# Norm sums as columns of numbers, spread to rows by TensorE, and a longer share of a convolution on VectorE

## The chip, the cores and the metric

The kernel runs on one core of a Trainium2 chip. The metric is the time of one execution in microseconds (us) on the device; a kernel is described by the median of its runs. A profiled execution is one more run, of which the hardware recorded every instruction. Its time is that of the whole run; its span, from the first to the last recorded work, is a little shorter.

## What is computed

Two blocks, each of two layers, on one sequence of 256 tokens with 1,024 features, all in float32. The change touches the seam between the blocks and the first mixer of the second block. Cut to that:

```python
# end of the first block: x = x + gate*y, then
x = rmsnorm(x, final_norm_g)              # per token: x / sqrt(mean(x*x)+eps) * g
# second block, layer 0
h = rmsnorm(x, norm_mix_g[0])             # again a norm per token, of the result above
p = h @ w_in_ab                           # 512 columns a, 512 values v, 512 gates g
ya = fnet_heads(p[..., :512], fnet_map)   # DFT over tokens and head, real part, a map
u = v * sigmoid(g)
u = conv(u, conv_w, 31 taps, pad 15, one filter per channel) + conv_b
u = silu(layernorm(u, per head of 128))   # four heads
y = concat([ya, u]) @ w_out_ab
x = x + y                                 # then the SwiGLU layer, and the second layer
```

## The kernel before

**Layout.** Activations lie with features on the 128 partitions and tokens along the row: a tile is 128 x 256, a tensor of 1,024 features is eight tiles `d`. In the second block's residual path the tokens lie on the partitions instead. Weights come as 128 x 2048 slabs (1 MB) by DMA into five `raw` buffers. ScalarE copies a slab to a rounded high half and VectorE subtracts to get the low half, both into one of four `W` buffers; each product is then three TensorE matmuls (high x high, high x low, low x high) on the rounded type. `stream` and `fill(k)` are the calls that do this splitting: `fill(k)` brings the engine up to slab k + 3 of the list of matrices. It stands by hand in the programs of ScalarE and VectorE, and a slab's split can't start before the slab four places ahead of it has been used up.

**Order.** There is no scheduler. Each engine has its own program, written out by hand, and runs it strictly in order; semaphores tie them together. `Port.wait_ge` drops waits already met. A matmul of plain float32 has two records in the trace, one of the rounded type has one. A PSUM bank (`pb0` to `pb7`) may be written when the name before it in that bank is free: `Outputs` hands out banks in a ring (`out`, `hold`) or by hand (`place`), and `freed(name)` says which semaphore frees it. `bank_free` on TensorE waits for that.

**The seam.** After the attention output (`project("ao", ...)` on VectorE) the first norm needs the sum of squares over all features of each token. ScalarE squares each tile, VectorE adds the eight squares (`add`), and TensorE multiplies with a matrix of ones (`row_sum`), so that all 128 partitions get the sum as a row of 256; ScalarE takes the root (`row_root`) and VectorE the reciprocal (`row_close`) of 128 x 256. `col_sums` gives the same sums as a column. Then X is scaled by gain and norm (eight operations, `s_x3`), squared and summed again for the second norm. Meanwhile TensorE already works on the unnormed product: `head(20, ...)` and `head(22, ...)` are slabs 20 to 23 (outputs `b` 0 to 7, gates and values), with the closing of the two sums (`close`) between the halves of each. Slabs 24 and 25 give `a` 0 to 3.

**The convolution.** Four tiles `d`, 31 taps. VectorE does taps as multiply-adds of 128 x 256 (`pump`), in the order of the list `taps`; the first tap of a tile is ScalarE's (`start_tap`). `NPE` taps of tile 2 and all of tile 3 are matmuls on TensorE (`convolved`) with diagonal matrices that ScalarE makes (`diagonals`). On TensorE the DFT matmuls (`ac`, `f`, `fm`) stand ahead of them. VectorE's `low(R1, h, fm)`, one for each of the four `fm` outputs, stands in the middle of the taps and counts up `s_flo`. Then each tile is normed per token: `ln_mean`, `ln_centre`, `ln_square`, `ln_var`, `ln_root`, `ln_scale`. `mixed` is the product with `w_out_ab`, `turn` a transpose of its sum.

## Time and profile before

| | us |
|---|---|
| median of 3 runs | 755.68 |
| lowest, highest | 754.87, 759.08 |
| the profiled execution, its own time | 755.56 |
| its span | 753.8 |
| TensorE matmuls busy | 721.7 (96%) |
| VectorE busy | 503.9 (67%) |
| ScalarE busy | 389.9 (52%) |

The share of an engine over the whole span is a mean over stages. In the stage that the change touches, from about 246 to 345 us of the span, all three engines have to be read beside each other, instruction by instruction. In a timeline a row gives the start, the length from first start to last end, engine, line of the code, operation, output <- inputs, shapes and the count of equal instructions that follow each other. Matmuls overlap in the pipeline, so what one costs is the distance between starts, not its length.

### The profile page before, as it was taken

How to read it: one execution, taken by the hardware profiler on the slowest of the kernel's cores; microseconds unless marked ns; L12 is line 12 of the kernel's file. 1: busy time of each engine (PE TensorE's matmuls, PEld its weight loads, DVE VectorE, ACT ScalarE, POOL GpSimd, SP SyncE). 2: the span in 40 equal slices, each digit the busy share in tenths (PEclk: the TensorE clock that was granted, in tenths of full speed). 3: DMA queues.
4: the chain of work that ended last, by engine and by line, in shares of the span. 5: the costliest groups of instructions: out<-in, count | busy, mean ns of one | idle time of the engine just before them, and what ended most of it. 6: DMA issues, size and time to landing. Idle time of an engine off the chain costs nothing.

```text
span 753.8 us, 9658 instructions
## 1 busy us (share of the span) xinstructions
PE 721.7 (96%) x3900; PEld 629.7 (84%) x3900; DVE 503.9 (67%) x760; ACT 389.9 (52%) x602; POOL 2.4 (0%) x8
## 2 busy tenths in 40 slices
PE   3999995999999999999999999999999999999996
PEld 2888885999999999888888888888888888888885
DVE  4866987986976789987664454555576554454444
ACT  4146526347675667846844434444466533434423
POOL 0000000000000000000000000000000000000000
PEclk9999998999999999999999999999999999999998
DMA  9999774796934434234364555545324455545201
GB/s 348 418 420 422 324 270 177 296 423 272 400 124 169 167 130 184 79 113 168 142 249 171 200 187 184 206 168 196 139 113 171 181 206 171 203 184 179 102 0 57
DMA packets 23085, 156.65 MB, mean 208 GB/s; under 512 B 2560, under 2 KB 2688, under 8 KB 5120
## 3 DMA queue, kind: packets, MB, share of 16 engines
q1 hardware_dynamic: 22464, 153.41, 53.6%
q0 software_dynamic: 576, 2.62, 1.0%
q8 instruction: 31, 0.51, 0.3%
q14 instruction: 14, 0.11, 0.0%
HBM read 154.97 MB, written 1.05 MB: 207 GB/s over the span
## 4 chain that ended last, share of the span: by engine, by line
PE 77%; DVE 10%; ACT 8%; DMA 3%; issue 1%; SPq 0%; DVEq 0%; ACTq 0%
PE pb L1454 19%; PE pb L1456 18%; PE pb L1455 18%; PE pb L1524 13%; DVE w L956 4%; PE pb L1683 2%; DVE raw L959 2%; DMA raw<-w_dram 2%; ACT w L593 2%; PE pb L1784 1%; ACT r L698 1%; ACT t L701 1%; PE pb L1530 1%; DVE rs L1015 1%; PE pb L1714 1%
## 5 line engine op out<-in xcount | busy, mean ns | idle before, releaser
L956 DVE TENSOR_TENSOR w<-raw,w 128x2048 fp32r<-128x2048 f32 x97 | 221.4, 2291 | 142.6 <-ACT w L593 142.5
L593 ACT ACTIVATE w<-raw 128x2048 fp32r<-128x2048 f32 x97 | 184.8, 1913 | 157.2 <-PE pb L1456 114.9
L1454 PE MATMUL pb<-w,r 128*128 128x512 f32 (+1 forms) x640 | 244.2, 381 | 0.7 <-DVE r L959 0.3
L1456 PE MATMUL pb<-w,r 128*128 128x512 f32 (+1 forms) x640 | 241.0, 377 | 0.0
L1455 PE MATMUL pb<-w,r 128*128 128x512 f32 (+1 forms) x640 | 240.6, 376 | 0.0
L1454 PEld LDWEIGHTS pb<-w,r 128*128 128x128 f32 x640 | 120.5, 188 | 23.1 <-issue 1.8
L1456 PEld LDWEIGHTS pb<-w,r 128*128 128x128 f32 x640 | 120.4, 188 | 22.5
L1455 PEld LDWEIGHTS pb<-w,r 128*128 128x128 f32 x640 | 120.6, 188 | 21.2
L1454 PE MATMUL pb<-r,w 128*128 128x256 f32 x352 | 101.6, 289 | 7.1 <-DVE r L956 6.6
L1455 PE MATMUL pb<-r,w 128*128 128x256 f32 x352 | 100.2, 285 | 0.0
L1456 PE MATMUL pb<-r,w 128*128 128x256 f32 x352 | 100.1, 284 | 0.0
L959 DVE SCALAR_TENSOR_TENSOR raw<-raw,acc 128x1024 f32<-128x1024 f32 x64 | 75.0, 1221 | 3.1 <-DMA raw<-w_dram 3.0
L1454 PEld LDWEIGHTS pb<-r,w 128*128 128x128 f32 x352 | 68.1, 194 | 8.1 <-issue 7.1
L1455 PEld LDWEIGHTS pb<-r,w 128*128 128x128 f32 x352 | 68.2, 194 | 0.1
L1456 PEld LDWEIGHTS pb<-r,w 128*128 128x128 f32 x352 | 68.1, 194 | 0.0
L1524 PE MATMUL pb<-h,ow 128*128 128x256 f32 x256 | 57.3, 387 | 3.5 <-ACT h L656 3.5
L1524 PEld LDWEIGHTS pb<-h,ow 128*128 128x128 f32 x256 | 49.7, 195 | 11.0 <-issue 3.9
L897 ACT ACTIVATE t<-pb,rn 128x256 f32<-128x256 f32 x44 | 20.7, 475 | 59.8 <-PE pb L1456 59.8
L959 DVE SCALAR_TENSOR_TENSOR f<-f,vec 128x256 f32<-128x256 f32 x102 | 42.4, 483 | 5.0 <-ACT f L661 4.6
L959 DVE SCALAR_TENSOR_TENSOR t<-pb,rn,t 128x256 f32<-128x256 f32 x44 | 21.1, 483 | 22.9 <-ACT t L897 22.9
L1524 PE MATMUL pb<-t,ow 128*128 128x256 f32 x128 | 27.8, 379 | 0.0
L1524 PEld LDWEIGHTS pb<-t,ow 128*128 128x128 f32 x128 | 24.3, 190 | 3.3
(174 smaller groups left out, 572.0 us busy)
## 6 DMA issues: line engine op xcount, KB each, us to landing
raw<-w_dram SPq DMA_DIRECT2D x129, 1024.0 KB, 4.9
ow<-w_dram SPq DMA_DIRECT2D x8, 1024.0 KB, 19.2
ow<-w_dram SPq DMA_DIRECT2D x8, 512.0 KB, 15.6
oh<-w_dram SPq DMA_DIRECT2D x2, 1024.0 KB, 21.5
x<-x_dram SPq DMA_DIRECT2D x2, 512.0 KB, 6.0
f<-rc_dram POOLq DMA_DIRECT2D x1, 1024.0 KB, 5.1
acc<-row_dram POOLq DMA_DIRECT2D x2, 512.0 KB, 5.4
out_dram<-f SPq DMA_DIRECT2D x4, 256.0 KB, 2.3
```

The costliest lines, as they stand in the source:

```text
L593: return e.activation(out, in_, ACT.Copy, **kw)
L698: e.activation(hi_of(R, kt), F3[:, kt, :], ACT.Identity, **kw).then_inc(done, 1)
L701: e.activation(tt[kt][:, :], F3[:, kt, :], ACT.Identity, **kw).then_inc(done, 1)
L897: e.activation(tt[(at_ - 1) % 4][:, :], bank_of("gu", layer, i, a)[:, 0:T], ACT.Silu, scale=rn[:, 2 * layer, a:a + 1]).then_inc(s_sgt, 1)
L956: return e.tensor_tensor(out, a, b, op)
L959: return e.scalar_tensor_tensor(out, a, s, b, op0, op1, **kw)
L1015: e.reciprocal(RS[{0: 0, 1: 1, 2: 0, 3: 1, 4: 0, 6: 1, 7: 0}[i]][:, :], root[:, :]).then_inc(s_rs, 1)
L1454: e.matmul(out, a_hi, b_hi, start=start, stop=False)
L1455: e.matmul(out, a_hi, b_lo, start=False, stop=False)
L1456: return e.matmul(out, a_lo, b_hi, start=False, stop=stop)
L1524: return e.matmul(out, slab[:, o:o + P], rhs, start=start, stop=stop)
L1683: done = e.matmul(out_of("cv", d), dg[n % 8], G0[:, d, j:j + T], start=j == 0, stop=j == count - 1)
```

## The change

The sums of squares between the blocks are no longer added on VectorE. ScalarE writes the eight squares to `SQ` (the buffer F2), and 16 small matmuls (`token_sums`) with the squares as stationary operand and a two-column operand `og` (ones, and the gain squared) give both sums, plain and gained, as columns of 128 x 2. The root, reciprocal and products are taken of 128 x 2 columns; the second norm's number is worked out from the first, so that the second pass of squares is gone. `spread` makes rows of the columns: a matmul of the column, broadcast to 128 x 128, with the identity. Four of them and one ScalarE copy fill `RS`. The same is done in the layer norms (`ln_var` of two columns, `lnr`, `ln_row`). `NPE` goes from 12 taps of tile 2 and 31 of tile 3 (43 matmuls) to 21 taps of tile 3; VectorE takes the rest. The orders of all three engines around it are rewritten, and `mixed` for slabs 28 and 29 is cut into more pieces.

```diff
-NPE = 12
-LN = (0, 1, 3, 2)
+NPE = 21
+FIRST_TAP = {0: 0, 1: 0, 2: 0, 3: NPE}
...
     o.hold(*run("b", 0, 1, 2, 3))
-    o.out(("n", 2), ("nc", 0))
+    o.out(("ns", 0))
     o.finish(*run("b", 0, 1, 2, 3))
+    o.out(("rb", 0))
...
     o.hold(*run("b", 4, 5, 6, 7))
-    o.out(("n", 3), ("nc", 1))
     o.finish(*run("b", 4, 5, 6, 7))
...
-    o.place(4, ("cv", 2), ("ln", 2))
+    o.place(4, ("ln", 2))
     o.place(5, ("cv", 3), ("ln", 3))
...
-        taps = [(d, j) for j in range(31) for d in (0, 1)] + [(2, j) for j in range(NPE, 31)]
+        taps = [(d, j) for j in range(11) for d in (0, 1)]
+        taps += [x for j in range(20) for x in ((0, 11 + j), (1, 11 + j), (2, j))]
+        taps += [x for j in range(11) for x in ((2, 20 + j), (3, NPE + j)) if x[1] < 31]
...
 # ScalarE
-            row_root(2)
-            col_root(0, rcol[:, 0:2])
+            sums = PB[OUT.bank["ns", 0]][:, 0:4].rearrange("p (a j) -> p a j", j=2)
+            p.wait_ge(*ended("ns", 0))
+            e.activation(rcol[:, 0:2], sums[:, :, 0], ACT.Sqrt, scale=1.0 / D, bias=V("eps", 0)).then_inc(s_rtc, 1)
+            p.wait_ge(s_col, 2)
+            e.activation(rcol[:, 2:4], rcol[:, 2:4], ACT.Sqrt, scale=1.0 / D, bias=V("eps", 0)).then_inc(s_rtc, 1)
             fill(20)
...
+            p.wait_ge(*ended("rb", 0))
+            copy(RSt[:, :, :], bank_of("rb", 0)[:, :].rearrange("p (a n) -> p a n", a=2)).then_inc(s_rsb, 1)
             fill(21)
...
+            p.wait_ge(s_gpad, 1)
             gated(0)
             gated(1)
+            start_tap(0)
+            start_tap(1)
+            fill(22)
             gated(2)
             gated(3)
-            p.wait_ge(s_gpad, 1)
-            start_tap(0)
-            start_tap(1)
+            start_tap(2)
+            start_tap(3)
...
 # VectorE
+            fill(20)
+            p.wait_ge(s_rsb, 1)
+            for d in range(8):
+                stt(X[:, d, :], X[:, d, :], V("final_norm_g", d), RS[0], MUL, MUL).then_inc(s_x3, 1)
...
             for d in range(2):
                 gated(d, F1[:, 6 + d, :], F1[:, 4 + d, :], (s_b, d + 1), (s_b, d + 3))
+            pump(10)
+            fill(21)
+            pump(12)
             for d in range(2, 4):
                 gated(d, out_of("b", 2 + d), out_of("b", 4 + d), ended("b", 2 + d), ended("b", 4 + d))
-            fill(22)
-            pump(12)
-            for c in range(2):
-                fill(24 + c)
-                pump(10)
-            for h in range(4):
-                pump(3)
-            pump(62 - tap_n["n"])
+            for k in range(22, 25):
+                fill(k)
+                pump(15)
             for h in range(4):
                 p.wait_ge(s_fhi, h + 1)
                 low(R1, h, out_of("fm", h), s_flo)
-                pump(2)
+                pump(4)
+            pump(2)
...
+            pump(4)
             ln_centre(0)
             ln_centre(1)
+            pump(6)
+            ln_inverse(0)
+            ln_inverse(1)
+            pump(4)
+            ln_scale(0)
+            ln_scale(1)
+            fill(25)
             pump(len(taps) - tap_n["n"])
...
 # TensorE
+            def spread(out, col):
+
+                return e.matmul(out, col.broadcast_to([P, P]), ident, start=True, stop=True)
...
+            def token_sums():
+
+                bank_free("ns", 0)
+                out = bank_of("ns", 0)
+                p.wait_ge(s_og2, 1)
+                for d in range(8):
+                    p.wait_ge(s_sq, 16 + d + 1)
+                    for a in range(2):
+                        done = e.matmul(out[:, 2 * a:2 * a + 2], SQ[:, d, a * P:a * P + P], og[:, d, :],
+                                        start=d == 0 and a == 0, stop=d == 7 and a == 1)
+                done.then_inc(s_ps, 1)
+
+            head(20, run("b", 0, 1, 2, 3), 0, token_sums)
+            bank_free("rb", 0)
+            p.wait_ge(s_col, 3)
+            for i, c in ((0, 0), (1, 4)):
+                for a in range(2):
+                    done = spread(bank_of("rb", 0)[:, i * T + a * P:i * T + a * P + P], rcol[:, c + a:c + a + 1])
+            done.then_inc(s_ps, 1)
+            pair(22, run("b", 4, 5, 6, 7), R2, s_rlo, 0, range(8))
...
+            bank_free("cv", 3)
+            p.wait_ge(s_gt, 12)
+            for j in range(NPE):
+                p.wait_ge(s_dg, j + 1)
+                done = e.matmul(out_of("cv", 3), dg[j % 8], G0[:, 3, j:j + T], start=j == 0, stop=j == NPE - 1)
...
-            ln_mean(2, (s_cv2, 1))
+            ln_mean(0, (s_tap, tap_at[0, 30]))
+            ln_mean(1, (s_tap, tap_at[1, 30]))
             mixed(0, 0, 0, 1)
             mixed(0, 1, 0, 1)
+            ln_var(0)
+            ln_var(1)
             mixed(1, 0, 0, 1)
...
             for a in range(2):
                 for c in range(2):
                     if a and c:
                         turn(0, 0)
-                    for kt in range(4, 8):
+                    for kt in (6, 7):
                         mixed(kt, c, a)
```

TensorE's program from the last DFT outputs (`fm`) to the means, of before. The names: `f0` holds the gated values, `acc1` the diagonals, `cst` the identity, `f1` the convolved tiles; in brackets the semaphores waited for ahead of the row.

```order
L1672 MATMUL pb6<-f2,cst 128x256 [waits s_f]
L1672 MATMUL pb7<-f2,cst 128x256 [waits s_f]
L1672 MATMUL pb0<-f2,cst 128x256 [waits s_f]
L1672 MATMUL pb1<-f2,cst 128x256 [waits s_f]
L1683 MATMUL pb4<-f0,acc1 128x256 [waits s_dg] x12
L1683 MATMUL pb5<-f0,acc1 128x256 [waits s_dg,s_gt]
L1683 MATMUL pb5<-f0,acc1 128x256 [waits s_dg] x19
L1689 MATMUL pb6<-f1,ones_sb 128x256 [waits s_tap,s_flo]
```

The same place of after:

```order
L1681 MATMUL pb4<-f2,cst 128x256 [waits s_f]
L1681 MATMUL pb5<-f2,cst 128x256 [waits s_f]
L1681 MATMUL pb6<-f2,cst 128x256 [waits s_f]
L1681 MATMUL pb7<-f2,cst 128x256 [waits s_f]
L1688 MATMUL pb5<-f0,acc1 128x256 [waits s_dg,s_gt,s_flo]
L1688 MATMUL pb5<-f0,acc1 128x256 [waits s_dg] x20
L1729 MATMUL pb0<-cst,x 128x128 [waits s_x3]
```

Two outputs fewer go through the ring of banks, so every later one lies two banks lower: `fm` 1, in bank 7 before, now lies in bank 5, which the convolution writes next, and the convolution's first matmul waits for the second count of `s_flo`; the means of tiles 0 and 1 stand behind all of it.

VectorE's program from the gate products to the second `low` of after (`t0` the gate, `f0` the gated values, `f1<-f0,vec,f1` a tap, `w<-raw,w` the low half of a slab, `rs` the norm's row):

```order
L947 TENSOR_TENSOR f0<-f0,t1 128x256 [waits s_gt,s_sg]
L950 SCALAR_TENSOR_TENSOR f1<-f0,vec,f1 128x256 [waits s_tap0]
L950 SCALAR_TENSOR_TENSOR f1<-f0,vec,f1 128x256 [waits s_tap0,s_gt]
L950 SCALAR_TENSOR_TENSOR f1<-f0,vec,f1 128x256 [waits s_tap] x6
L947 TENSOR_TENSOR w2<-raw1,w2 128x2048 [waits s_hi]
L950 SCALAR_TENSOR_TENSOR f1<-f0,vec,f1 128x256 [waits s_tap] x12
L947 TENSOR_TENSOR t2<-pb2,rs 128x256 [waits s_ps]
L947 TENSOR_TENSOR f0<-pb0,rs 128x256
L947 TENSOR_TENSOR f0<-f0,t2 128x256 [waits s_gt,s_sg]
```

Of before, the slab 24 (`w2<-raw1`) is split ahead of this place, and the gate products of tiles 2 and 3 follow at once on those of tile 1; eight and twelve taps and that slab now stand between them.

ScalarE's program at the sigmoids, before and then after (`root`, `rcol` the norm's roots, `w<-raw` the high half of a slab, `t0` the gate):

```order
L593 ACTIVATE w3<-raw2 128x2048 [waits s_raw2]
L790 ACT_TABLE_LOAD
L790 ACTIVATE t0<-t0 128x256 [waits s_gt]
L790 ACTIVATE t1<-t1 128x256 [waits s_gt]
L790 ACTIVATE t2<-t2 128x256 [waits s_gt]
```

```order
L603 ACTIVATE rs<-pb7 128x512 [waits s_ps]
L603 ACTIVATE w2<-raw1 128x2048 [waits s_raw1]
L787 ACT_TABLE_LOAD [waits s_gt]
L787 ACTIVATE t0<-t0 128x256 [waits s_gpad]
L787 ACTIVATE t1<-t1 128x256 [waits s_gt]
```

With two waits ahead of the sigmoid, the table load now stands behind the wait for the gate product (`s_gt`).

## Rows read from the trace of the kernel before

**Rows 1.** The page, busy us by engine with share and instructions

```profile
PE 721.7 (96%) x3900; PEld 629.7 (84%) x3900; DVE 503.9 (67%) x760; ACT 389.9 (52%) x602; POOL 2.4 (0%) x8
```

**Rows 2.** Busy us of PE, PEld, DVE, ACT, POOL in a stretch; clock, DMA

```profile
308.00:322.00 14.00, 14.00 (x67) 12.25 (x66) 13.96 (x37) 13.52 (x36) 0.00 (x0) 1.00 0.02 9
```

**Rows 3.** TensorE's timeline at the first row and column sums

```profile
264.88 0.28 PE L1519 MATMUL pb<-ones_sb,na 128*128 128x1 f32 x2
265.02 0.36 PE L1520 MATMUL pb<-ones_sb,na 128*128 128x1 f32 x2
...
265.45 0.28 PE L1455 MATMUL pb<-r,w 128*128 128x256 f32 x1
265.57 0.28 PE L1456 MATMUL pb<-r,w 128*128 128x256 f32 x1
```

**Rows 4.** TensorE's weight loads at the same place

```profile
265.00 0.30 PEld L1520 LDWEIGHTS pb<-ones_sb,na 128*128 128x128 f32 x2
265.22 0.19 PEld L1454 LDWEIGHTS pb<-r,w 128*128 128x128 f32 x1
```

**Rows 5.** VectorE's timeline from the first norm to the first transposes

```profile
265.64 1.75 DVE L1015 RECIPROCAL rs<-root 128x256 f32<-128x256 f32 x1
...
269.75 1.27 DVE L959 SCALAR_TENSOR_TENSOR x<-x,vec,rs 128x256 f32<-128x256 f32 x3
271.11 0.42 DVE L956 TENSOR_TENSOR na<-na,sq 128x256 f32<-128x256 f32 x1
...
293.56 4.49 DVE L956 TENSOR_TENSOR w<-raw,w 128x2048 fp32r<-128x2048 f32 x2
...
304.12 15.93 DVE L959 SCALAR_TENSOR_TENSOR f<-f,vec 128x256 f32<-128x256 f32 x40
319.95 0.43 DVE L956 TENSOR_TENSOR r<-pb,r 128x256 fp32r<-128x256 f32 x1
...
344.43 6.69 DVE L956 TENSOR_TENSOR w<-raw,w 128x2048 fp32r<-128x2048 f32 x3
```

**Rows 6.** ScalarE's timeline at the sigmoids, the first taps and later

```profile
280.27 1.28 ACT L790 ACT_TABLE_LOAD   x1
282.87 0.42 ACT L790 ACTIVATE t<-t 128x256 f32<-128x256 f32 x1 [1.32 <-DVE t L956]
...
286.93 1.08 ACT L795 ACTIVATE f<-f,vec 128x256 f32<-128x256 f32 x2
...
380.44 0.60 ACT L593 ACTIVATE r<-pb 128x512 fp32r<-128x512 f32 x1
```

**Rows 7.** TensorE's timeline from the DFT to the second transposes

```profile
295.60 3.62 PE L1657 MATMUL pb<-cst,f 128*128 128x256 f32 x16
...
307.69 13.98 PE L1683 MATMUL pb<-f,acc 128*128 128x256 f32 x64
...
327.12 1.95 PE L1726 MATMUL pb<-cst,x 128*128 128x128 f32 x16
...
338.02 0.70 PE L1693 MATMUL pb<-t,ones_sb 128*128 128x256 f32 x2 [0.87 <-ACT t L840]
...
353.09 0.39 PE L1455 MATMUL pb<-w,r 128*128 128x512 f32 x1
353.31 0.39 PE L1456 MATMUL pb<-w,r 128*128 128x512 f32 x1
353.55 1.03 PE L1714 MATMUL pb<-cst,x 128*128 128x128 f32 x8
...
359.88 1.03 PE L1714 MATMUL pb<-cst,x 128*128 128x128 f32 x8
```

**Rows 8.** TensorE after its longest wait: timeline row, then busy and clock

```profile
125.53 0.55 PE L1454 MATMUL pb<-r,w 128*128 128x256 f32 x1 [6.40 <-DVE r L956]
...
125.00:127.00 2.00, 1.47 (x7) 0.50 0.04 8
127.00:129.00 2.00, 2.00 (x12) 0.59 0.00 0
```

More of the change, by code:

```diff
@@ L350, in two_block_program @@
         root = sb("root", [P, T])
-        RS = [sb(f"rs{i}", [P, T]) for i in range(2)]
-        NA = [sb(f"na{i}", [P, T]) for i in range(2)]
+        RSt = sb("rs", [P, 2, T])
+        RS = [RSt[:, i, :] for i in range(2)]
+        NA = sb("na", [P, T])
         mv = sb("mv", [P, 12, 8])
@@ L628, in row_root @@
                 e.activation(root[:, :], out_of("n", i), ACT.Sqrt, scale=1.0 / D, bias=V("eps", 0)).then_inc(s_rt, 1)
-            def col_root(c, out):
-                p.wait_ge(*ended("nc", c))
-                e.activation(out, PB[OUT.bank["nc", c]][:, 0:2], ACT.Sqrt, scale=1.0 / D,
-                             bias=V("eps", 0)).then_inc(s_rtc, 1)
             def raw_high(r, R, d, gain):
@@ L831, in _ @@
                 if h < 3:
-                    diagonals(2, range(2 * h, 2 * h + 2))
-            start_tap(2)
+                    diagonals(2 * h, 2 * h + 1)
             for h in range(4):
@@ L867, in _ @@
                 copy(hi_of(R1, 4 + d), tt[4 + d][:, :]).then_inc(s_cs2, 1)
+            diagonals(*range(6, 14))
+            fill(25)
+            diagonals(*range(14, NPE))
+            fill(26)
+            for ds in ((0, 1), (2, 3)):
+                for d in ds:
+                    ln_square(d)
+                for d in ds:
+                    ln_root(d)
+                for d in ds:
+                    ln_high(d)
             fill(27)
@@ L1125, in _, with project @@
                     y_tile(d)
-            def project(kind, i, done, scale, before, raw_, streams):
+            def project(kind, done, scale, before, raw_, streams):
                 for d in range(8):
@@ L1138, in project @@
                         stt(X[:, d, :], out_of(kind, d), scale(d), X[:, d, :], MUL, ADD).then_inc(done, 1)
-                    if d >= 2:
-                        add(i, d - 1)
+                    if raw_ is None and d >= 2:
+                        add(d - 1)
                     if raw_ is not None and d:
@@ L1688, in ln_mean, with ln_row @@
                 p.wait_ge(*sums)
-                e.matmul(PB[OUT.bank["ln", d]][:, 0:T], ones, F1[:, d, :], start=True, stop=True).then_inc(s_lnm, 1)
+                e.matmul(bank_of("ln", d)[:, 0:T], ones, F1[:, d, :], start=True, stop=True).then_inc(s_lnm, 1)
             def ln_var(d):
-                p.wait_ge(s_lnq, LN.index(d) + 1)
-                e.matmul(PB[OUT.bank["ln", d]][:, 256:512], ones, tt[d][:, :], start=True,
-                         stop=True).then_inc(s_lnv, 1)
-            convolved(2, NPE, range(NPE))
-            convolved(3, 31, range(0, 20))
-            ln_mean(0, (s_tap, tap_at[0, 30]))
-            ln_mean(1, (s_tap, tap_at[1, 30]))
-            convolved(3, 31, range(20, 31))
+                p.wait_ge(s_lnq, d + 1)
+                for a in range(2):
+                    done = e.matmul(bank_of("ln", d)[:, T + a:T + a + 1], tt[d][:, a * P:a * P + P], ones_sb[:, 0:1],
+                                    start=True, stop=True)
+                done.then_inc(s_lnv, 1)
+            def ln_row(d):
+                p.wait_ge(s_lni, d + 1)
+                for a in range(2):
+                    done = spread(bank_of("ln", d)[:, T + a * P:T + a * P + P], lnr[:, d, a:a + 1])
+                done.then_inc(s_lnb, 1)
             def wide(k, o, R, r, a, out, start, stop):
```

254 lines of the change are left out of this document (104 added, 150 removed).

## The prediction, made before the change was run

> **What bounds the kernel now.** I read the page first: TensorE is busy for 721.7 of the span's 753.8 us, VectorE for 503.9 [rows 1]. That says TensorE, and the waits that end on TensorE agree: in the stage of the change the longest is 0.87 us [rows 7]. Then the stretches: from 308 to 322 us TensorE is busy for 14.00 us of 14 and VectorE for 13.96 [rows 2]. Two engines are full there, and which of them is late is decided by order, not by load. So I read the timelines and wrote the new orders out against them, with the durations of the old.
>
> **What goes from TensorE.** A float32 matmul of 256 columns costs 0.432 us: 32 of them (64 records) last 13.98 us, less a tail of 0.15 [rows 7]. Of 128 columns it is half, 0.217. The convolution loses 22, 9.5 us. Two closings of 0.80 go (a row sum, 0.43, and two column sums, 0.37): 1.6. Four variances of 0.43: 1.7. Together 12.9 us.
>
> **What comes to it.** Sixteen token sums with two columns each, and eight column sums in the layer norms. The nearest row has one column: the loads of one such matmul and of the next start 0.22 us apart (265.00, 265.22) [rows 4]. The starts of the two matmuls lie 0.14 apart (264.88, 265.02) [rows 3], and the load row is 0.30 long [rows 4]. I take 0.22, since with so few columns the load is what repeats; 0.14 and 0.30 are the ends. That makes 3.5 us (2.2 to 4.8) and 1.8 us (1.1 to 2.4). Twelve spreads of 128 columns: 2.6. Together 7.9. On TensorE alone the change is worth 12.9 - 7.9 = 5.0 us, and 1.2 more if its small waits go too.
>
> **What goes from and comes to VectorE.** Fourteen additions at about 0.34 (4.8), two norm reciprocals of 128 x 256 and four in the layer norms at 1.66 (10.0; the row's 1.75 less overlap), against 21 multiply-adds at 0.398 (40 last 15.93) [rows 5]: 8.4. VectorE too has 6 us less to do. What matters is when it does it.
>
> **The new order, step by step, in the time of the old trace.**
>
> 1. TensorE reaches the first sums as before, 0.43 ahead of 264.88, at 264.45 [rows 3]. The squares are there: VectorE no longer adds between. Sums 3.5: 267.95. The second half of slabs 20 and 21 is 48 products at 0.12 (265.45, 265.57) [rows 3], 5.8: 273.7. The column numbers take seven short hops between VectorE and ScalarE meanwhile, about 2 us, and are hidden by these 5.8. Four spreads, 0.9: 274.6.
> 2. ScalarE copies 128 x 512, 0.60 [rows 6], with handing over 275.3. Only now may VectorE scale X; before it began at 269.75 [rows 5]. Eight operations at 0.395 (three last 1.27) [rows 5], 3.2: 278.5.
> 3. One gate product, 0.34. Before, the sigmoid's table load (1.28) was over when its product came [rows 6]. Now it stands behind the wait for the product, so load and sigmoid are both exposed: 1.28 + 0.42 [rows 6]. With the rest of the gates of tiles 0 and 1 (1.5) it is 282.2, and ScalarE's first tap (two last 1.08) [rows 6] lets VectorE start at 282.8.
> 4. From there to the second `low` VectorE has 68 taps (27.1), four slabs at 2.2 (two last 4.49, three 6.69) [rows 5], 8.8, the gates of tiles 2 and 3 (2.3) and two `low` (0.43 each) [rows 5]: 39.0. It ends at 321.8.
> 5. TensorE meanwhile: slabs 22 and 23 are 96 products, 286.1. Slab 24's low half stands behind the first eight taps: 282.8 + 3.2 + 2.2 = 288.2, a wait of 2. Slab 25's stands behind twelve taps and the gates of tiles 2 and 3: 297.5, while TensorE is there at 294.0, a wait of 3.6. Then 5.8 for that slab and 28 matmuls of the DFT (12.1): 315.6. There the convolution's first matmul waits for the second `low`, because its bank is the one of `fm` 1: until 321.9, 6.2 us. The two slab waits cost nothing by themselves, since this one swallows them.
> 6. The convolution so starts at 321.9, before at 307.69 [rows 7]: 14.2 us late. Queued behind its wait on TensorE are 21 convolution matmuls, the transposes of X into the sum, and the means of tiles 0 and 1; VectorE, ahead in its taps, soon stands before `ln_centre(0)`, waiting for those means, for 5 to 6 us. That is what turns its lighter load into nothing.
> 7. To the first transpose (`turn`), before 353.55 - 307.69 = 45.9 us [rows 7]. Now 21 x 0.432 = 9.1; transposes of X 3.5 (16 records last 1.95) [rows 7]; four means 1.7; 90 products of 512 columns at 0.227 (353.09 and 353.31 are two in a row, rounded) [rows 7], 20.4; column sums 1.8; spreads 1.7: 38.2. Two waits come on top. The mean of tile 2 waits for its last tap: VectorE has by then the scaling of tiles 0 and 1, a slab and four taps to do after 342.3, so 346.9, TensorE is there at 345.3: 1.7. And `turn` waits for X, which VectorE copies only behind two slabs (4.4, ScalarE's half ahead of them 1.8) that start when the last layer-norm tile is done, at 358.4. With X's copy (0.6) it is 365.2. Before, 36 products of 512 columns lay between the norms and `turn`; now 18. TensorE is there at 361.8: 3.4. So `turn` is at about 365.2, 11.6 late.
> 8. From this turn to the next, 6.33 before [rows 7], six products fewer: 5.2, by the splits and copies of X between. 1.1 comes back: 10.5 late. Behind that the programs are the same, and I carry it to the end.
> 9. The clock. After the wait of 6.40 us at 125.53 TensorE's granted clock is 0.50 in one stretch and 0.59 in the next [rows 8], that is 1.2 GHz for about 2.3 us, then full speed again. That loses 1.1 us. The wait of step 5 is as long, and TensorE is what is late after it. The cost is between 0 and, with the later waits, 1.5; I take 1.1, its nearest row.
>
> **The sum.** 10.5 + 1.1 = 11.6 us. The profiled execution took 755.56 us, 0.12 from the median of the runs, so it can stand for them: 767.2.
>
> ScalarE's table load is a term of step 3 by its row, 1.28 us. The Trainium skill (ScalarE: Activation LUTs, What ACT_TABLE_LOAD costs) puts the price of a load at about 2.7 us; by that the exposed load would add 1.4 and the time would be 768.6. The sum goes by the trace, which has 1.28 us at each of the loads shown.
>
> For the token sums the Trainium skill (TensorE: Matmul & The Clock Gate, Back-to-back issue gap) gives some 60 cycles for a matmul of 1 to 64 columns, 25 ns. An estimate from that, two passes each, would be 0.8 us in place of 3.5 for the sixteen, and 764.5. No row here comes near it.
>
> **Rivals.**
>
> *TensorE bounds it throughout* (7%). For it: both engines have less to do, and in the old stretch VectorE kept up. Then 5.0 + 1.2 go, 749.4. It needs VectorE at the second `low` by 309.7 (274.6 + 23.0 + 12.1), 12 us earlier than step 4; its 39 us would have to be 27. Nothing in the rows makes a tap a third cheaper.
>
> *The wait at the bank is met, the rest stands* (10%). If VectorE is some 6 us quicker from 269 to 322, or TensorE so much later, steps 5 and 9 fall: 767.2 - 6.2 - 1.1 = 759.9. For it: four hops of mine are estimates. Against: the taps are 27 of the 39 us, and their price has 40 instructions in one row.
>
> *The clock doesn't fall and the sums are at 0.14* (part of the forecast's range): 767.2 - 1.1 - 1.9 = 764.2.
>
> *Dearer sums and clock* (part of it too): at 0.30 the sums add 1.9 and the later waits 0.4: 769.5.
>
> **How the numbers follow.** My forecast, 767.2 with its own range from 763 to 770.5, has a chance of 79%; 10% for the bank wait met, 7% for TensorE throughout, 4% for a mixture that ends within half a per cent of before. Half a per cent, 3.8 us, is about what a measurement of this kernel can tell from no change. So faster has 0.07, the same 0.04, slower 0.89. The range that should hold the time 8 times in 10 reaches down to the second case and a little over the upper end: 760 to 771.
>
> **What would show it.** TensorE's timeline should have a wait of about 6 us ahead of the first convolution matmul, ended by VectorE's `low`; waits of about 2 and 3.6 us ahead of slabs 24 and 25, ended by VectorE's slab; some 3 us ahead of the first `turn`. VectorE should stand 5 to 6 us before `ln_centre(0)`, and ScalarE should load a table right after the first gate product. The sixteen sums should take 3.5 us. The granted clock should show 1.2 GHz for some 2 us behind the long wait. I am wrong if TensorE has no long wait there, or if the time lost is given back in the gate and up products of the next stage.

## The result, and the profile of the changed kernel

| | before | changed |
|---|---|---|
| median, us | 757.34 (4 runs) | 771.07 (4 runs) |
| lowest, highest, us | 754.87, 759.08 | 770.30, 773.13 |
| profiled execution, own time | 755.56 | 773.13 |
| its span | 753.8 | 771.2 |

The ratio is 1.019, with a 95% interval from 1.015 to 1.023: slower by 14 us. The forecast was 767.2 with a range from 760 to 771; the median lies just above its top. The direction was right, the size too small. In the later series, of 7, 18 and 13 runs, the kernel before has medians of 755.97, 755.56 and 755.09, so the 757.34 of four runs is rather high, and the loss is nearer to the 15 us that the stations below give.

The page of the changed kernel, busy time by engine. TensorE should have had 5 us less to do than in [rows 1]; it shows 3.7 more, although VectorE has 6.7 less:

```profile
PE 725.4 (94%) x3908; PEld 631.8 (82%) x3908; DVE 497.2 (64%) x768; ACT 381.6 (49%) x573; POOL 2.4 (0%) x8
```

Busy time is no measure of work when the clock changes below it, so the timelines decide. The two programs are the same up to the seam, yet this profiled execution comes to the first sums at 266.80, the one of before at 264.45. I count everything from there; the last section tells of the 2.35 us.

TensorE's timeline of the changed kernel: the token sums, the spreads, slabs 24 and 25, the convolution, the transposes of X, the means of tiles 0, 1 and 2, the two turns. In brackets the wait ahead and what ended it:

```profile
266.80 3.63 PE L1648 MATMUL pb<-og,f 128*128 128x2 f32 x32
277.61 1.05 PE L1515 MATMUL pb<-cst,rcol 128*128 128x128 f32 x8
292.28 0.39 PE L1455 MATMUL pb<-r,w 128*128 128x256 f32 x1 [2.10 <-DVE w L947]
301.72 0.39 PE L1455 MATMUL pb<-r,w 128*128 128x256 f32 x1 [3.43 <-DVE w L947]
325.79 11.02 PE L1688 MATMUL pb<-f,acc 128*128 128x256 f32 x42 [4.48 <-DVE r L947]
336.64 3.73 PE L1729 MATMUL pb<-cst,x 128*128 128x128 f32 x32
340.21 1.03 PE L1694 MATMUL pb<-f,ones_sb 128*128 128x256 f32 x4
352.92 1.13 PE L1694 MATMUL pb<-f,ones_sb 128*128 128x256 f32 x4 [1.60 <-DVE f L950]
371.72 1.23 PE L1721 MATMUL pb<-cst,x 128*128 128x128 f32 x8 [2.87 <-DVE x L1351]
377.31 1.03 PE L1721 MATMUL pb<-cst,x 128*128 128x128 f32 x8
```

In [rows 7] the convolution stands without a wait; here it has one, ended by VectorE's `low` (`r`, L947), and 42 records take 11.02 us where 64 took 13.98.

VectorE's timeline: it scales X only from 279.33 (before from 269.75, [rows 5]); the second `low` ends at 325.73 and lets the convolution start; then VectorE stands for 7.48 us before `ln_centre(0)`, waiting for the means that queue behind the convolution:

```profile
279.33 3.26 DVE L950 SCALAR_TENSOR_TENSOR x<-x,vec,rs 128x256 f32<-128x256 f32 x8 [3.56 <-ACT rs L603]
284.75 0.42 DVE L947 TENSOR_TENSOR f<-f,t 128x256 f32<-128x256 f32 x1 [1.49 <-ACT t L787]
325.32 0.41 DVE L947 TENSOR_TENSOR r<-pb,r 128x256 fp32r<-128x256 f32 x1
340.85 0.86 DVE L950 SCALAR_TENSOR_TENSOR f<-pb,f 128x256 f32<-128x256 f32 x2 [7.48 <-PE pb L1694]
```

ScalarE's timeline at the first sigmoid. In [rows 6] the load is over before the product comes; here it starts only behind it:

```profile
283.00 1.28 ACT L787 ACT_TABLE_LOAD   x1 [1.90 <-DVE t L947]
284.30 0.42 ACT L787 ACTIVATE t<-t 128x256 f32<-128x256 f32 x1
```

Busy time in stretches (PE, PEld, DVE, ACT, POOL), the clock in the third column from the end. TensorE is busy without a gap from 266 to 278, and yet its clock falls to half, behind the token sums; then behind the wait ahead of slab 25, for which the forecast had no fall; then again at the convolution, behind the wait:

```profile
268.00:270.00 2.00, 2.00 (x20) 2.00 (x19) 0.00 (x0) 0.00 (x0) 0.00 (x0) 1.00 0.67 279
270.00:272.00 2.00, 2.00 (x16) 2.00 (x17) 0.91 (x7) 0.91 (x3) 0.00 (x0) 0.87 0.54 221
272.00:274.00 2.00, 2.00 (x12) 2.00 (x11) 0.56 (x2) 1.44 (x1) 0.00 (x0) 0.50 0.00 0
274.00:276.00 2.00, 2.00 (x15) 2.00 (x15) 1.77 (x1) 0.00 (x0) 0.00 (x0) 0.78 0.00 0
...
302.00:304.00 2.00, 2.00 (x12) 2.00 (x12) 2.00 (x7) 2.00 (x3) 0.00 (x0) 0.55 0.58 152
304.00:306.00 2.00, 2.00 (x13) 2.00 (x12) 2.00 (x7) 0.23 (x1) 0.00 (x0) 0.60 0.88 373
...
326.00:328.00 2.00, 2.00 (x6) 1.62 (x6) 2.00 (x7) 0.77 (x2) 0.00 (x0) 0.52 0.00 0
328.00:330.00 2.00, 2.00 (x8) 1.59 (x7) 2.00 (x7) 0.90 (x4) 0.13 (x1) 0.62 0.00 0
```

The stations, in us behind the first sums. "Before" is the old kernel, "forecast" the prediction's times less 264.45.

| station | before | forecast | measured |
|---|---|---|---|
| first spread | | 9.25 | 10.81 |
| VectorE scales X | 5.3 | 10.85 | 12.53 |
| second `low` ends | | 57.35 | 58.93 |
| convolution starts | 43.24 | 57.45 | 58.99 |
| transposes of X begin behind it | | 67.65 | 69.84 |
| mean of tile 0 | | 71.1 | 73.41 |
| first turn | 89.10 | 100.75 + 1.1 for the clock | 104.92 |
| second turn | 95.43 | 105.9 + 1.1 | 110.51 |

So the seam lost 15.1 us where 11.6 were forecast. The spans say the same: 17.4 apart, less the 2.35 from ahead of the seam.

### The profile page after: what moved, and what is told of

It is laid out like the page before. It is cut to its first block, busy times and chain, and to the rows that moved or that the text cites. A ratio compares the mean times of both kernels' runs of the same rounds, so it can differ in the third digit from the quotient of the medians.

```text
span 771.2 us, 9627 instructions
## 1 busy us (share of the span) xinstructions
PE 725.4 (94%) x3908; PEld 631.8 (82%) x3908; DVE 497.2 (64%) x768; ACT 381.6 (49%) x573; POOL 2.4 (0%) x8
## 3 DMA queue, kind: packets, MB, share of 16 engines
HBM read 154.97 MB, written 1.05 MB: 202 GB/s over the span
## 4 chain that ended last, share of the span: by engine, by line
PE 73%; DVE 15%; ACT 8%; DMA 3%; issue 1%; SPq 0%; ACTq 0%; DVEq 0%
PE pb L1455 18%; PE pb L1457 18%; PE pb L1456 18%; PE pb L1519 13%; DVE w L947 5%; DVE f L950 4%; DVE raw L950 2%; DMA raw<-w_dram 2%; ACT w L603 2%; PE pb L1688 1%; PE pb L1800 1%; ACT r L697 1%; ACT t L700 1%; PE pb L1525 1%; PE pb L1721 1%
## 5 line engine op out<-in xcount | busy, mean ns | idle before, releaser
L947 DVE TENSOR_TENSOR w<-raw,w 128x2048 fp32r<-128x2048 f32 x97 | 221.5, 2290 | 144.0 <-ACT w L603 144.0
L1455 PE MATMUL pb<-r,w 128*128 128x256 f32 x352 | 103.1, 293 | 12.0 <-DVE r L947 6.4
L1456 PE MATMUL pb<-r,w 128*128 128x256 f32 x352 | 101.6, 289 | 0.0
L1457 PE MATMUL pb<-r,w 128*128 128x256 f32 x352 | 101.5, 288 | 0.0
L1455 PEld LDWEIGHTS pb<-r,w 128*128 128x128 f32 x352 | 69.6, 198 | 13.0 <-issue 6.8
L1456 PEld LDWEIGHTS pb<-r,w 128*128 128x128 f32 x352 | 69.8, 198 | 0.1
L1457 PEld LDWEIGHTS pb<-r,w 128*128 128x128 f32 x352 | 69.6, 198 | 0.0
L950 DVE SCALAR_TENSOR_TENSOR f<-f,vec 128x256 f32<-128x256 f32 x123 | 50.1, 477 | 9.1 <-ACT f L660 8.8
L603 ACT ACTIVATE f<-pb 128x256 f32<-128x256 f32 x44 | 15.9, 386 | 23.1 <-PE pb L1457 12.6
```

The source lines that it names most:

```text
L603: return e.activation(out, in_, ACT.Copy, **kw)
L947: return e.tensor_tensor(out, a, b, op)
L950: return e.scalar_tensor_tensor(out, a, s, b, op0, op1, **kw)
L1455: e.matmul(out, a_hi, b_hi, start=start, stop=False)
L1456: e.matmul(out, a_hi, b_lo, start=False, stop=False)
L1457: return e.matmul(out, a_lo, b_hi, start=False, stop=stop)
```

## The experiments

The theory after this comparison has three parts. VectorE is what is late, and the wait at the convolution's bank turns its lateness into TensorE's. The way of the norm is the root: sums, clock and spreads delay VectorE's start. The layer norms cost nothing. The rival is that the change's many small matmuls on TensorE, or the moved slabs and taps, cost by themselves wherever the bank lies. Times are medians; the ratio is against runs of the kernel before on the same chip. Stations are counted from the first sums. In e4_inter, e8_fixed and e10_best these stand at another place of the program; there I count from the start of slab 20, with the 5.76 us added that lie between it and the first sums in the changed kernel.

**e1_bank: the ring of banks moved on by two**, so that `fm` 1 and the convolution no longer share bank 5.

```diff
     o.slab(23, ("b", 7))
+    o.n += 2
     for c in range(2):
```

> The changed kernel with one line more: the ring of banks is advanced by two ahead of the outputs a, so that everything behind lies two banks higher and the convolution's bank was last used by f, not by fm. All times from the first token sum. Theory (the convolution waits for VectorE's second low only because of its bank, and the clock falls behind that wait): the wait of 4.48 us ahead of the convolution is gone, it starts at 54.5 and not 59.0, at full clock, and lasts 9.1 and not 10.9; the identity matmuls then wait for the fourth low (62.8) and start about 63 and not 69.8; the first turn is 6 to 6.5 us earlier; 765 us. Rival (VectorE is late anyway, what is gained ahead of the convolution is lost at the means and at turn): the first turn moves by less than 2 us, 769.5 us or more.

Measured: 764.60 (763.75 to 765.92), ratio 1.011 [1.008, 1.014], 6.5 us below the changed kernel. TensorE's timeline at the convolution has no wait left, and 42 records cost what the clock at full speed makes of them:

```profile
320.43 9.23 PE L1689 MATMUL pb<-f,acc 128*128 128x256 f32 x42
```

The second turn is at 104.02 behind the first sums, 6.5 earlier than in the changed kernel: 4.5 of wait and 1.8 of clock. VectorE's stand before `ln_centre(0)` falls from 7.48 to 1.05. The bank is worth 6.5 us; 8.6 remain.

Here the rival gets its due, for with the bank free TensorE's own time counts. The convolution starts 11.1 later than before. By the distances of starts, 2.7 of it is work (sums and spreads 4.3 for two closings of 1.6), 1.5 the clock behind the sums (48 products in 7.3, not 5.8), 5.2 the two slab waits, 1.5 the clock behind the second of them (7.35 us for slab 25's products instead of 5.86), 10.9 in all. From its start to the second turn 49.7 us pass, before 52.2: 2.5 come back.

**e2_slabs: VectorE's splits of slabs 24 and 25 (`fill(21)`, `fill(22)`) ahead of the taps**, which takes away the two waits at slabs 24 and 25.

```diff
-            pump(10)
             fill(21)
+            pump(10)
+            fill(22)
             pump(12)
...
-            for k in range(22, 25):
+            pump(15)
+            for k in range(23, 25):
```

> The changed kernel with VectorE's splits of slabs 24 and 25 ahead of the first ten and twelve taps and not behind them, nothing else. Theory (the waits of 2.1 and 3.4 us ahead of these slabs cost nothing by themselves, since TensorE would only wait longer ahead of the convolution): both waits gone or below 0.5 us, the wait ahead of the convolution grows from 4.5 to about 9.5 us, its start stays within 0.5 us, time within 1 us of the changed kernel. Rival (they are 5.5 us of the loss): 765.5 us.

Measured: 771.82, one run; beside it the changed kernel's median of 771.07. Both slab waits are gone and the wait at the bank has grown from 4.48 to 8.40: VectorE has the same work to do up to its second `low`, and TensorE is merely there sooner (the convolution starts at 58.56, was 58.99). One more wait, 2.38, came ahead of the DFT:

```profile
302.96 1.97 PE L1668 MATMUL pb<-cst,f 128*128 128x256 f32 x8 [2.38 <-ACT f L603]
...
324.24 11.14 PE L1690 MATMUL pb<-f,acc 128*128 128x256 f32 x41 [8.40 <-DVE r L947]
```

The second turn is at 110.37 instead of 110.51. As long as the bank wait stands behind them, the slab waits cost nothing by themselves, as step 5 said.

**e3_load: the pad's wait moved behind the first two sigmoids**, so that the table load stands ahead of the wait for the product again.

```diff
-            p.wait_ge(s_gpad, 1)
             gated(0)
             gated(1)
+            p.wait_ge(s_gpad, 1)
             start_tap(0)
```

> The changed kernel with ScalarE's wait for the cleared margins moved behind the first two sigmoids, so that one wait stands ahead of the first sigmoid and the table load isn't behind it. Theory (the load is exposed on VectorE's path to the second low): VectorE's wait for the first sigmoid falls from 1.49 to about 0.2 us, the convolution starts 1.3 us earlier (57.7 us from the first token sum and not 59.0), the time is 1.3 us lower. Rival (hidden): no change of the convolution's start.

Measured: 773.31, one run. The wait at the first sigmoid is gone and the convolution starts 1.35 us earlier, 57.64 behind the first sums. But the second turn is at 110.64, no earlier than before the edit. TensorE's timeline and the stretches show where the gain went:

```profile
324.32 10.93 PE L1688 MATMUL pb<-f,acc 128*128 128x256 f32 x38 [5.96 <-DVE r L947]
...
370.97 1.94 PE L1721 MATMUL pb<-cst,x 128*128 128x128 f32 x8 [2.86 <-DVE x L1351]
```
```profile
324.00:326.00 2.00, 1.68 (x4) 1.41 (x5) 2.00 (x6) 0.40 (x1) 0.00 (x0) 0.50 0.00 0
326.00:328.00 2.00, 2.00 (x6) 1.55 (x6) 2.00 (x6) 0.80 (x2) 0.00 (x0) 0.50 0.00 0
328.00:330.00 2.00, 2.00 (x8) 1.65 (x7) 1.93 (x6) 1.13 (x4) 1.05 (x2) 0.67 0.42 66
```

The convolution lasts 11.6 us from its start to the transposes, 0.8 more than in the changed kernel, because the clock is down for longer; and at the first turn the clock is down too (1.94 us where the changed kernel has 1.23). The turn after it then comes 6.35 behind, where the changed kernel has 5.59. The table load is a real term of step 3, but its 1.3 us were not gained here: the clock took them back at both places. With one run each, why the clock was down at the turn in this run and not in the changed kernel stays open.

**e4_inter: the token sums in four portions**, two tiles behind each of the column blocks 3 to 6 of slabs 20 and 21, instead of all eight behind the fourth. The work is the same. The core of the edit; `token_sums` takes the tiles as its argument:

```diff
-            head(20, run("b", 0, 1, 2, 3), 0, token_sums)
+            for kt in range(8):
+                pair(20, run("b", 0, 1, 2, 3), R2, s_rlo, 0, range(kt, kt + 1), first=kt == 0, last=kt == 7)
+                if kt in (2, 3, 4, 5):
+                    token_sums({2: (0, 1), 3: (2, 3), 4: (4, 5), 5: (6, 7)}[kt])
```

> The changed kernel with the sixteen token sums spread between the products of slabs 20 and 21, four of them behind each of the third to sixth feature tile, and not in one block of 3.6 us. Theory (the granted clock fell behind the block because TensorE did only tiny matmuls in it): no stretch from 264 to 278 us shows a clock under 0.95, and the four spreads end about 1.4 us earlier than in the changed kernel, counted from the start of slab 20; the convolution starts 1 to 1.4 us earlier, time 770. Rival (the clock falls whatever the order): a mean clock near 0.83 from the sums on, no gain.

Measured: 769.96, one run. Busy time in stretches:

```profile
262.00:274.00 12.00, 12.00 (x105) 12.00 (x104) 3.47 (x8) 3.92 (x6) 0.00 (x0) 1.00 0.33 126
274.00:298.00 24.00, 20.29 (x166) 19.71 (x165) 20.33 (x45) 11.32 (x16) 0.00 (x0) 1.00 0.26 88
298.00:306.00 8.00, 5.67 (x28) 5.67 (x29) 8.00 (x17) 5.02 (x7) 0.00 (x0) 0.57 0.37 131
```

The clock stays at 1.00 through the sums and until slab 25, and the time from the start of slab 20 to the first spread is 15.07 us where it was 16.57: 1.5 less, which is the gap between forecast and measurement at that station. Only half of it reaches VectorE, which scales X 0.8 earlier (11.76), behind a slab's split that now ends last; the convolution starts 0.8 earlier too. The wait at the bank is 3.65, the clock behind it stays up (9.2 from the convolution's start to the transposes, was 10.85), and the second turn is at 107.95, 2.5 earlier: 0.8 by the earlier start and 1.7 by the clock at the convolution. The third stretch is slab 25, behind a wait of 3.43; its products take 8.2 us at the lower clock, and the bank wait swallows that. The fall of the clock behind the sums in one block is shown; it had no term in my sum.

**e5_ring: the kernel before with the ring moved on by six**, which is its state of banks in the changed kernel and nothing else of it.

```diff
     o.slab(23, ("b", 7))
+    o.n += 6
     for c in range(2):
```

> The kernel before with one line more: the ring of banks is advanced by six (that is, two back) ahead of the outputs a, so that the convolution's two banks were last used by fm 0 and fm 1 as in the changed kernel; nothing else. Theory (the place in the ring alone makes TensorE wait for VectorE's low): a wait of about 12.5 us ahead of the first convolution matmul, ended by VectorE's low, clock at half speed behind it, the first turn 13 to 14 us later than before, time 769 to 770 us. Rival (the long wait belongs to the new tap order, not to the bank): no wait, 756 us.

Measured: 769.99, one run, beside 755.56 for the kernel before. The wait ahead of the convolution alone, with norms, taps and orders of before:

```profile
320.38 14.86 PE L1684 MATMUL pb<-f,acc 128*128 128x256 f32 x60 [12.58 <-DVE r L957]
```
```profile
310.00:322.00 12.00, 1.62 (x4) 1.36 (x5) 11.96 (x32) 0.36 (x1) 0.00 (x0) 0.50 0.00 0
```

The second turn is at 109.92, 14.5 later than before. One number in the plan of banks makes as much loss as the whole change. It is more than the 6.5 of e1_bank because TensorE comes here on time, at 307.8, and VectorE's `low` only at 319.95, as in [rows 5]; the clock adds the rest.

**e6_norm: the new way of the norm alone**, on the kernel before, with the ring moved by two so that the bank wait can't arise. The layer norms and the 43 matmuls of the convolution stay as before. With the norm, VectorE's order had to move: the gates of tiles 2 and 3 stand behind 22 entries of the tap list. The run prices the two together. The core of the edit:

```diff
-            head(20, run("b", 0, 1, 2, 3), 0, lambda: close(2, 0))
-            head(22, run("b", 4, 5, 6, 7), 0, lambda: close(3, 1))
+            head(20, run("b", 0, 1, 2, 3), 0, token_sums)
+            bank_free("rb", 0)
+            p.wait_ge(s_col, 3)
+            for i, c in ((0, 0), (1, 4)):
+                for a in range(2):
+                    done = spread(bank_of("rb", 0)[:, i * T + a * P:i * T + a * P + P], rcol[:, c + a:c + a + 1])
...
```

> One part alone: the kernel before with the norms between the blocks as columns (token sums, spreads, ring kept two higher so that the convolution's banks are free), the convolution, its taps and the layer norms as before; the gate products of tiles 2 and 3 and slab 25 stand behind 22 entries of the tap list, since their inputs come later. Theory (the column form costs by itself, since VectorE can't scale X before TensorE has run the second half of slabs 20 and 21, 10 us later than before, and the clock falls behind the sums): the first turn 6 to 8 us later than before, 763 us. Rival (the loss comes from the taps and the bank): within 2 us of before.

Measured: 765.00 (763.46 to 767.04), ratio 1.013 [1.010, 1.016]. TensorE's timeline: the sums, the spreads, and a wait of 3.54 ahead of slab 24 for VectorE's gates:

```profile
263.33 4.12 PE L1641 MATMUL pb<-og,f 128*128 128x2 f32 x32
275.70 1.05 PE L1508 MATMUL pb<-cst,rcol 128*128 128x128 f32 x8
...
297.56 0.55 PE L1448 MATMUL pb<-r,w 128*128 128x256 f32 x1 [3.54 <-DVE f L952]
```
```profile
266.00:268.00 2.00, 2.00 (x12) 2.00 (x12) 0.19 (x2) 0.26 (x1) 0.00 (x0) 0.58 0.79 328
268.00:270.00 2.00, 2.00 (x11) 2.00 (x11) 0.76 (x6) 1.63 (x2) 0.00 (x0) 0.50 0.00 0
270.00:272.00 2.00, 2.00 (x12) 2.00 (x11) 1.50 (x1) 0.47 (x1) 0.00 (x0) 0.50 0.00 0
```

The spread is 12.37 behind the first sums, the convolution starts at 53.42 (before 43.24), and the second turn is 10.2 late: all of the loss lies ahead of the convolution. This one part costs 10 us where it was meant to take work away; I had expected 6 to 8. Against the kernel before, the 10.2 are made up of 2.7 of work on TensorE (as in e1_bank), 3.1 of clock at and behind the sums (in the changed kernel 1.5), 3.2 of wait (3.54 for 0.37) and 1.2 of clock behind that wait. So more than half of it, 5.8, is TensorE's own time, and only 4.4 comes from VectorE being late. The rival, that the small matmuls cost by themselves, is right for that part.

**e7_ln: the layer norms as columns alone**, on the kernel before.

```diff
...
-                e.matmul(PB[OUT.bank["ln", d]][:, 256:512], ones, tt[d][:, :], start=True,
-                         stop=True).then_inc(s_lnv, 1)
+                for a in range(2):
+                    done = e.matmul(bank_of("ln", d)[:, T + a:T + a + 1], tt[d][:, a * P:a * P + P],
+                                    ones_sb[:, 0:1], start=True, stop=True)
+                done.then_inc(s_lnv, 1)
...
+            ln_row(0)
+            ln_row(1)
```

> One part alone: the kernel before with the layer norms of the convolution as columns (eight matmuls of one column, roots and reciprocals of 128 x 2, eight spreads), all else as before. Theory (TensorE bounds this stretch and has 1.8 us more to do, while the 6.6 us that VectorE saves lie beside its work): between the same and 2 us slower, 756.5 to 758. Rival (VectorE's reciprocals are on the path): 752 to 754.

Measured: 756.01 (754.88 to 758.84), ratio 1.001 [0.999, 1.003]; the second turn is at 96.16, 0.7 late. It takes four reciprocals of 128 x 256 from VectorE, which isn't late there. On TensorE column sums and spreads take 3.2 us for the 1.7 of the variances that they replace, 1.5 more, and the wait of 0.87 from [rows 7] is gone: what is left fits the 0.7. In the times no difference can be measured.

**e8_fixed: the repairs together** (e1_bank, e2_slabs, e3_load, e4_inter), and 26 taps on TensorE instead of 21, to take some of the work off VectorE.

```diff
-NPE = 21
+NPE = 26
...
```

> The changed kernel with all four faults mended at once: ring advanced by two, slabs 24 and 25 split ahead of the taps, table load ahead of the first gate product, token sums between the products; and 26 taps of tile 3 on TensorE and not 21. Theory (the gains add, VectorE is then the later engine by its start at the first tap): the first turn 8 to 9 us earlier than in the changed kernel, 758 to 760 us, not below the kernel before. Rival (with the faults gone the lighter load of both engines shows): 752 us or less.

Measured: 760.55 (757.85 to 764.27), ratio 1.008 [1.006, 1.010]. The second turn is 4.5 later than before. Its waits are 0.92 and 1.86 at the slabs and 2.87 at the first turn. The first turn is 11.8 earlier than in the changed kernel, more than the 8 to 9 expected, but 1.2 are lost at once: the clock is 0.50 from 362 to 364 us, and the next turn comes 6.81 behind, not 5.59.

**e9_early: spreads earlier**, on top of e1_bank. If VectorE's start is what counts, then the 24 products between the columns and the spreads cost as much as they last.

```diff
...
+                if kt == 5:
+                    spreads()
...
```

> The changed kernel with the ring moved by two banks (as e1_bank) and with the four spreads of the first norm moved from behind slabs 20 and 21 to behind the sixth of their eight column blocks; ScalarE copies the spread out ahead of the slabs' banks. Theory: what puts the convolution late, once the bank is out of it, is how late VectorE may begin to scale X. It begins 24 products at 0.12, 2.9 us, earlier, the waits ahead of slabs 24 and 25 shrink by as much, and the second turn is 2 to 3 us nearer: 2 to 2.9 us below e1_bank, ratio about 1.008. Rival: VectorE's start is not what counts, because TensorE's own work and its clock behind the sums set the place of the convolution: then the waits move and the time stays within 0.8 us of e1_bank, ratio about 1.011.

Measured: 762.73 (760.94 to 763.44), ratio 1.009 [1.006, 1.012]; the second turn is at 101.95, 2.07 earlier than in e1_bank. TensorE's timeline, the spreads now 7.97 behind the first sums:

```profile
263.18 3.87 PE L1645 MATMUL pb<-og,f 128*128 128x2 f32 x32
271.15 1.05 PE L1516 MATMUL pb<-cst,rcol 128*128 128x128 f32 x8
...
296.03 0.39 PE L1456 MATMUL pb<-r,w 128*128 128x256 f32 x1 [3.43 <-DVE w L948]
```

VectorE scales X 2.84 earlier (9.69 instead of 12.53), loses 0.77 of it at the sigmoids (2.26 instead of 1.49, since ScalarE's copies now stand ahead of the load), and the remaining 2.07 arrive whole at the second turn. The wait at slab 24 is gone. The one at slab 25 stayed at 3.43, which my expectation had wrong: TensorE came earlier by the same amount as VectorE. The times of the runs, 1.9 us apart, are too close for a proof by themselves; the stations agree with the theory and not with the rival. On TensorE the gain is the wait at slab 24, 2.10 in e1_bank.

**e10_best: all repairs, the early spreads, and 24 taps on TensorE.**

> The changed kernel with all repairs together: ring moved by two banks, the first sigmoids not held back by the pad's wait, slabs 21 and 22 ahead of taps, token sums spread behind column blocks 2, 3 and 4 of slabs 20 and 21, the spreads behind the sixth, and 24 taps of the convolution on TensorE instead of 21. Theory: the waits ahead of slabs 24 and 25 are all but gone and the clock stays up; against e8_fixed the spread is 2.9 us earlier and TensorE has two taps (0.9 us) less: 2 to 4 us below e8_fixed, ratio 1.001 to 1.005. Rival: with 24 taps VectorE is late again ahead of the convolution's end and the turn, and the gain goes into waits there: ratio 1.007 or above.

Measured: 758.30 (756.73 to 760.82), ratio 1.004 [1.002, 1.006], against 755.09 for the kernel before on the same chip. Up to the first turn the clock stays up, as the first two stretches show; behind the turn it falls, as the third does. The timeline shows the two longest waits that are left:

```profile
262.00:274.00 12.00, 12.00 (x106) 12.00 (x105) 4.87 (x10) 5.91 (x7) 0.00 (x0) 1.00 0.32 117
274.00:334.00 60.00, 58.17 (x382) 54.14 (x381) 57.17 (x127) 35.88 (x70) 1.05 (x2) 1.00 0.32 115
...
360.00:362.00 2.00, 2.00 (x6) 1.62 (x5) 1.66 (x7) 1.34 (x6) 0.00 (x0) 0.50 0.96 401
```
```profile
295.34 0.35 PE L1458 MATMUL pb<-r,w 128*128 128x256 f32 x1 [1.52 <-DVE f L948]
...
358.05 1.22 PE L1728 MATMUL pb<-cst,x 128*128 128x128 f32 x8 [2.86 <-DVE x L1354]
```

Of the 15.1 us at the second turn 11.9 are repaired, 3.2 are left. The clock behind the first turn has 1.2 of it: the second comes 6.78 behind the first, where the changed kernel, with nearly the same wait and no fall, has 5.59. The other 2.0 lie under the waits of 1.52 and 2.86 and some smaller ones; no run takes them apart. No version here beats the kernel before. Whether the wait at the first turn can go too wasn't tried.

**What it adds up to.** The ring costs 6.5 us (e1_bank), the norm's new way alone 10 (e6_norm), the layer norms under 1 (e7_ln). They sum to 17, the change costs 14 to 15: the shorter convolution on TensorE gives some 2 to 3 back. No run has the shorter convolution alone, and that number is the difference of the others; the 2.5 that come back behind the convolution's start in e1_bank, with the layer norms' 0.7 already taken off, agree with it. The parts don't add up cleanly either, since the clock behind the sums cost 3.1 in e6_norm and 1.5 in the changed kernel.

## What the prediction had right, and the steps that failed

Three steps failed, 3.5 us together. Step 1 put the clock behind the token sums at nothing; it cost 1.55. Step 9 priced the clock behind the bank wait at 1.1; it cost 1.75. Steps 7 and 8 counted every product at the price of one in a row and came 1.2 short.

**The mechanism held.** The places named all showed: the bank of `fm` 1, VectorE's `low` as what ends the wait, the slab waits of 2 and 3.6 (2.10 and 3.43), the exposed table load, the mean of tile 2 (1.60 for 1.7), the first turn (2.87 for 3.4), VectorE's stand before `ln_centre(0)` (7.48 for 5 to 6). The loss at the second turn was 15.1 where 11.6 were forecast. e5_ring and e1_bank show the bank from both sides.

**Step 1: sums right, clock missing.** The sixteen sums last 3.63 where 3.5 were taken by the load distance of [rows 4]. But the 5.8 us of products behind them were counted at full clock. They took 1.5 more, since part of them ran at half clock; e4_inter, with the sums spread out, has the first spread 1.5 earlier. Everything that depends on VectorE moved by that: the first spread, the scaling, the second `low`, the convolution, all 1.5 to 1.7 late against the forecast.

**Steps 2 to 4** held: from the first spread to the second `low` 48.12 us, forecast 48.10. That it fits so closely is luck: up to the first tap 8.9 us passed where 9.1 were forecast, from there 39.2 where 39.0 were. Three sums of the working are off by 0.1 or 0.2 as well (12.9 for 12.8 us of work that goes from TensorE, 282.2 for 282.0 in step 3, 315.6 for 315.4 in step 5); none of them matters to the outcome.

**Step 5: the wait at the bank was 4.48, not 6.2**, because TensorE came later. It reached slab 25 1.9 later than forecast, and needed 19.6 us from there instead of 18.1 at a clock that fell behind that wait too. The convolution's start didn't move by that, since VectorE sets it. That second fall of the clock, behind a wait of 3.43, had no term either; here it was hidden.

**Step 9: 1.1 for the clock should have been 1.75.** From the convolution's start to the transposes 10.85 us passed where 9.1 were counted. My nearest row was [rows 8], and I read it too short. At 0.50 from 125.53 to 127 and 0.59 over the next 2 us it has 1.5 + 1.6 = 3.1 us at half clock, not 2.3, and so a loss of 1.5, not 1.1. Read rightly it leaves 0.2 of the 0.65 to the difference between the two places.

**Steps 7 and 8: small gaps had no term.** From the mean of tile 0 to the second turn 37.1 us passed, forecast 35.9. A change from plain float32 to rounded matmuls costs 0.08 to 0.20: in the changed kernel, the product behind the means starts the next one after 0.43 us, not 0.23:

```profile
340.89 0.59 PE L1455 MATMUL pb<-w,r 128*128 128x512 f32 x1
341.32 0.40 PE L1456 MATMUL pb<-w,r 128*128 128x512 f32 x1
341.55 0.40 PE L1457 MATMUL pb<-w,r 128*128 128x512 f32 x1
```

The change cuts `mixed` into more pieces and so has more such changes. But the trace gives them only part of the 1.2. From the first mean to the second turn the 108 products take 2.3 us more than 0.227 each: 0.8 at the seven changes, the rest mostly around the waits. The means, sums, spreads and waits took 1.0 less than counted. No run takes these apart.

**The sum of the misses** is 1.55 (clock behind the sums) + 0.65 (clock behind the bank) + 1.2 to 1.3 (gaps) = 3.5 us, the distance from 11.6 to 15.1.

**The prices of the Trainium skill.** The table load took 1.28 us at the place where it was exposed, as in [rows 6]. The Trainium skill (ScalarE: Activation LUTs, What ACT_TABLE_LOAD costs) has the same for the load itself, 1283 ns; the 2.7 of the prediction is its price of a whole switch, with a drain of 1380 ns. That drain doesn't show here: the sigmoid starts 0.02 behind the load (284.28, 284.30), and e3_load, which takes the load off the path, starts the convolution 1.35 earlier. With 2.7 the prediction would have added 1.4 to a step that the trace has right. The floor of 25 ns for a matmul of 1 to 64 columns in the Trainium skill (TensorE: Matmul & The Clock Gate, Back-to-back issue gap) would by an estimate have made 0.8 of the sums; they took 3.63, each with a weight load of its own.

**The rivals.** TensorE as the bound throughout is refuted by all waits. "The bank wait is met" didn't come by itself; e1_bank made it, and what then remained was 8.6 us where that rival said 4.3 (759.9): it left out the clock behind the sums (1.5), the clock behind the wait at slab 25 (1.5), which no bank wait hid any more, and the gaps (1.2), and counted with a VectorE that is faster, not with a bank that is free. The range ended at 771 because its upper end took dearer sums and at most 1.5 for the clock, behind waits; a fall of the clock without a wait wasn't in it.

## What to carry to other kernels

An output fewer in a ring of banks moves every later one: look at who now shares a bank with whom, and what that name waits for, before counting instructions. A sum that goes from two engines to a third is not cheaper if it is more work there and closes later: in e6_norm 5.8 of 10.2 us were TensorE's own work and clock, and 4.4 came of what starts behind the sum (here VectorE's scaling). And of the orders tried here, many matmuls of two columns did better between wide ones than in a block.

## What the runs showed of the hardware that was not expected

- TensorE's clock fell to 1.2 GHz (granted 0.50) without a gap in its work: behind 3.6 to 4.1 us of matmuls of two columns, each with its own weights, in the changed kernel, e1_bank, e2_slabs, e3_load, e6_norm and e9_early. In e4_inter, e8_fixed and e10_best, with the same matmuls between wide products, it stayed at 2.4 GHz. The cost was 1.5 to 3.1 us.
- Waits of nearly the same length had different results. Behind 3.65 us (e4_inter, the bank) the clock stayed up, behind 4.48 it fell. At slab 25, behind 3.43 it fell (0.83 from 300 to 310 in the changed kernel), behind 3.44 in e3_load it stayed at 1.00. At the first turn, behind 2.86 to 2.88, it fell in e3_load, e8_fixed and e10_best and not in the changed kernel, e1_bank, e2_slabs, e4_inter and e9_early. So the length of the wait alone doesn't decide it in these runs.
- Identical programs differ at the start. The profiled executions reach the first sums at times from 263.18 (e9_early) to 266.80 (the changed kernel), though TensorE's program is the same ahead of them. In the changed kernel's the clock from 18 to 25 us was 0.56, in that of before (first sums at 264.45) it was 0.76, and in the three earliest (e6_norm, e7_ln, e9_early, at 263.18 to 263.33) 1.00. That the one makes the other is not shown. The changed kernel's row:

```profile
18.00:25.00 7.00, 5.11 (x12) 4.12 (x13) 6.90 (x17) 1.20 (x2) 0.00 (x0) 0.56 1.02 424
```

So a profiled execution's own time can be 2 us off for a reason that lies ahead of the edit; distances from a common station are the better measure.
